# Two moved calls in the attention loop: the first turn of cached keys, and the scores of the samples

## The chip, the cores and the metric

The kernel runs on one core of a Trainium2 chip. The core has five engines with an instruction queue each: TensorE (PE, matrix products; its weight loads are shown apart as PEld), VectorE (DVE), ScalarE (ACT), GpSimd (POOL) and SyncE (SP, which here issues nearly all transfers). They run side by side and wait for each other through semaphores. The metric is the device time of one execution in microseconds (us), the median of several.

## The reference, cut to what matters

Two layers of a hybrid decoder run for 256 prompt tokens and for 32 sample tokens (8 sequences of 4). Each layer mixes tokens in three ways, of which dilated attention is one, and projects all three back. What the changed lines compute:

```python
for g in range(ATT_N_GROUPS):                      # three groups, dilations 1, 4, 16
    qg = rms_norm(att[:, :, g, 0], q_norm[g])
    kg = rms_norm(att[:, :, g, 1], k_norm[g])
    vg = att[:, :, g, 2]
    if kv_bufs is None:                            # prompt
        o, lse = dilated_attention_prompt(qg, kg, vg, ATT_DILATIONS[g])
    else:                                          # samples: keys and values from a cache
        o, lse = dilated_attention_sample(qg, kg, vg, kv_bufs[g], ATT_DILATIONS[g])
    outs.append(o)
    lses.append(lse)
wts = jax.nn.softmax(jnp.stack(lses), axis=0)
y_att = jnp.sum(wts[..., None] * jnp.stack(outs), axis=0)
...
mixed = (gates[:, :, 0] * (y_hg @ w_out_hg)
         + gates[:, :, 1] * (y_ssm @ w_out_ssm)
         + gates[:, :, 2] * (y_att @ w_out_att))
```

A query sees 129 keys per group at the distances 0, dil, ..., 128 dil. A feed-forward stage follows, dense in layer 0 and with 8 experts in layer 1.

## The kernel before

Every engine's instructions are written out in order by hand; nothing reorders them later. Where two engines share a buffer, the later one waits for a semaphore. All products land in eight PSUM banks (2 KB per partition each). A table (`job(key, b)`) gives each result its bank; `open_bank(key)` makes PE wait until the previous content of that bank has been read out ("drained"), `close_bank` tells the readers that it is filled.

The changed loop stands in `mixer` on PE and runs once in each of the two layers. It makes four passes, n = 0, 2, 4, 6. A pass handles two heads of a block of 128 prompt queries (n and n + 1) and the cached keys of two sample sequences (n and n + 1):

- `scores(L, n, k)`: six products for two heads against the prompt's key block k, one head into bank 0 and one into bank 1. Passes 0 and 4 have only block 0 (`blocks_of(n)` is 1), passes 2 and 6 have blocks 0 and 1. Both blocks use the same two banks, so block 1 waits until DVE has read block 0 out.
- `sample_keys(L, b, k)`: turns (transposes) a part of sequence b's cached keys, k = 0 to 3, into banks 5, 6, 5, 6. Part 0 is two turns, the others are four each. Part 0 waits for the transfers of that sequence's cache (semaphore k_in). DVE reads parts 0 and 1 out, ACT parts 2 and 3.
- `sample_scores(L, pair)`: the sample queries against the turned keys of the two sequences of the pass before, into banks 7 and 3, which stay open over all four passes. It waits until all eight parts of these keys have been read out.
- `turn_weights`: turns the prompt's softmax weights, in banks 2 and 0; `weigh(L, n - 2)`: multiplies the weights of the pass before with the values, into bank 4.
- `out_tile(0, m)`, `out_tile(1, m)`: a 128-wide tile of the output projection of the two other branches, eight matmul rows in the trace, mostly in bank 1, which it shares with the second head's scores. They are work that PE can do while the softmax runs.

DVE's order (`prompt_scores`, the call for even n) in a pass is: read out the scores of block 0 of both heads with scale and mask (line 2780), then those of block 1 if there is one; the row maxima (2785, 2786); the key parts 0 and 1 of sequence n out of banks 5 and 6 (2766, 2768); the two sums' reciprocals and the scaling of the weights (2791, 2792), behind ACT's exponentials; and then `gated(0, n)`, which reads the out tile from bank 1 and multiplies it with its gate (2463). For odd n it is key parts 0 and 1, and `gated`. ACT's order is: the exponentials of both heads, key parts 2 and 3 of sequence n, the turned weights, key parts 2 and 3 of sequence n + 1. A key's buffers are three sequences deep. SP loads the caches of sequences 0 to 2 ahead of the loop, and that of sequence b after part 3 of sequence b - 3 has been turned.

PE's products all go through the helper line 1036 and its full-width turns through line 1042, so the trace tells them apart by shape: scores have 64-row weights, sample scores `128*32` weights, `weigh` `128*64` weights, out tiles `128x288`. A float32 product is two matmul rows in the trace, a turn is one.

Of the kernel before, what the change touches and what calls it, by code (L numbers as in the profile page):

```python
# [93 lines left out]
def hybrid_decoder(nc, x_prompt, x_sample, state_hgrn, state_ssm, state_conv, cache_kv_w128, cache_kv_w512,  # L94
# [6 lines left out]
    with ctx:  # L101
# [252 lines left out]
        def blocks_of(n):  # L354

            return 1 + n // 2 % 2
# [155 lines left out]
        def drained(key):  # L512
            b, n = jobs[key]
            return bank_drained[b], n + 1
# [33 lines left out]
        def cache_buffer(which, b):  # L548
            return (VALUE_BUFFER if which else KEY_BUFFER)[b]

        def cache_in(L, which, b):

            order = KEY_BUFFER + VALUE_BUFFER
            n = DB * which + b
            i = order[n]
            return k_in[i], 64 * (L * order.count(i) + order[:n + 1].count(i))
# [461 lines left out]
        def _(pe):  # L1018
# [4 lines left out]
            def open_bank(key):  # L1023

                b, n = jobs[key]
                assert opened[b] == n, key
                opened[b] += 1
                if n > 0:
                    pe.wait_ge(bank_drained[b], n)
                return bank[b]  # L1030

            def close_bank(ins, key):
                ins.then_inc(bank_filled[jobs[key][0]], 1)

            def put(out, lhsT, rhs, start=True, stop=True):
                return mm(out, lhsT, rhs, start=start, stop=stop, skip_group_check=True)  # L1036

            def turn(out, in_):

                k, m = in_.shape  # L1040
                if m == P:
                    return nc.tensor.transpose(out, in_, ident[0:k, 0:k])  # L1042
                return put(out, in_, ident[0:k, 0:k])
# [13 lines left out]
            def run(products):  # L1057
                for _ in products:
                    pass
# [27 lines left out]
            def mean_over_features(L, which):  # L1087
                acc = open_bank(("norm", L, which))
                pe.wait_ge(*at_norm("x_summed", L, which))
                close_bank(put(acc[:, 0:T], ones[:, :], hT[:, 0, :]), ("norm", L, which))  # L1090
# [332 lines left out]
            def scores(L, n, k):  # L1423

                j, tb = n // 4, n // 2 % 2
                both = [open_bank(("sc", L, n + e, k)) for e in range(2)]
                for g in range(AG):
                    for e in range(2):
                        r = slice(64 * e, 64 * e + 64)
                        ins = put(both[e][:, P * g:P * g + P], att[r, 4 * g + j, P * tb:P * tb + P],  # L1430
                                  att[r, 4 * g + 2 + j, P * k:P * k + P])
                        if g == AG - 1:
                            close_bank(ins, ("sc", L, n + e, k))
# [28 lines left out]
            def sample_keys(L, b, k):  # L1462

                rows, far = kb_rows[cache_buffer(0, b)], kb_far[cache_buffer(0, b)]
                acc = open_bank(("kT", L, b, k))
                if k == 0:
                    pe.wait_ge(*cache_in(L, 0, b))
                    for p in range(2):
                        ins = turn(acc[:, P * p:P * p + P], rows[:, 0, P * p:P * p + P])
                elif k < 3:  # L1470
                    for i in range(4):
                        r, p = 2 * (k - 1) + i // 2, i % 2
                        ins = turn(acc[:, P * i:P * i + P], rows[:, 1 + r, P * p:P * p + P])
                else:
                    for i in range(4):
                        ins = turn(acc[:, P * i:P * i + P], far[:, i // 2, P * (i % 2):P * (i % 2) + P])
                close_bank(ins, ("kT", L, b, k))
# [118 lines left out]
            def mixer(L):  # L1596
                for t in range(N_PROJ):
                    run(proj_tile(L, t))
                    if t == 0:
                        pe.wait_ge(consts_ready, 2)  # L1600
                        mean_over_features(L, 0)
                    if t == 1 and L == 0:
                        skip_columns()
                    run(small_products(L, t))
                    if t == AT_DT:
                        pe.wait_ge(wdt_in, 16 * (L + 1))
                        step_widths(L)
                    if t == AT_DT + 2:
                        acc = open_bank(("dt_sum", L))
                        pe.wait_ge(*drained(("dt", L)))  # L1610
                        close_bank(put(acc[0:SH, 0:T], fourth[:, :], yall[:, 9, :]), ("dt_sum", L))
                kv_rows_of(L)
                def out_tile(br, m):

                    n = n_slab[0] + 2 * br + m // 4
                    if m % 4 == 0:
                        pe.wait_ge(slab_in[n % RING], 16 * slab_dmas[n])
                    key = ("out", L, br, m)
                    close_bank(contract(key, slab(n, 4, 4 * P), P * (m % 4), 4, yall[:, 4 * br:4 * br + 4, :]), key)

                pe.wait_ge(*at("hg_done", L))
                pe.wait_ge(*at("ssm_done", L))
                for n in range(0, 8, 2):
                    scores(L, n, 0)
                    sample_keys(L, n, 0)
                    sample_keys(L, n, 1)
                    if blocks_of(n) == 2:
                        scores(L, n, 1)
                    if n > 0:
                        sample_scores(L, n // 2 - 1)  # L1630
                        weigh(L, n - 2)
                    out_tile(0, n)
                    sample_keys(L, n, 2)
                    sample_keys(L, n, 3)

                    sample_keys(L, n + 1, 0)
                    turn_weights(L, n, 0)
                    sample_keys(L, n + 1, 1)
                    if blocks_of(n) == 2:
                        turn_weights(L, n, 1)  # L1640
                    out_tile(0, n + 1)
                    turn_weights(L, n + 1, 0)
                    sample_keys(L, n + 1, 2)
                    if n < 6:
                        out_tile(1, n // 2)
                    if blocks_of(n) == 2:
                        turn_weights(L, n + 1, 1)
                    sample_keys(L, n + 1, 3)
                weigh(L, 6)
                sample_scores(L, 3)  # L1650
                for m in (3, 4, 5):
                    out_tile(1, m)
                sample_weights(L)
                out_tile(1, 6)
                sample_new_values(L)
                for pair in range(4):
                    sample_values(L, 2 * pair)
                    sample_values(L, 2 * pair + 1)
                    if pair > 0:
                        sample_heads(L, pair - 1)  # L1660
                sample_heads(L, 3)
                out_tile(1, 7)
                pe.wait_ge(*drained(("att_o", L, 1)))
                pe.wait_ge(*drained(("oT", L)))
                if L == DEPTH - 1:
                    pe.sem_inc(loop_signals["m_slab"], 16)
                n_slab[0] += 4
                proj_slab(L, [("out", L, 2, m) for m in range(KT)], 2, yall[:, 8:10, :])
                for s in range(NS_WO):
                    w = take_slab(KT, 256)  # L1670
                    for i in range(2):
                        key = ("wo", L, 2 * s + i)
                        acc = open_bank(key)
                        for k in range(KT):
                            if s == 0 and i == 0:
                                pe.wait_ge(*at("mixed_ready", L, k + 1))
                            ins = put(acc[:, 0:T], w[:, k, P * i:P * i + P], yall[:, k, :], k == 0, k == KT - 1)
                        close_bank(ins, key)
                        if L == DEPTH - 1 and s == 0 and i == 0:
                            pe.sem_inc(loop_signals["m_slab"], 2)  # L1680
                        m = 2 * s + i
                        if L == DEPTH - 1 and m > 0:
                            router_tile(m - 1)
                    n_slab[0] += 1
                if L == DEPTH - 1:
                    router_tile(KT - 1)
# [1672 lines left out]
```

## Time and profile before

| | us |
|---|---|
| median of 3 runs | 2120.06 (2118.96 to 2120.28) |
| profiled execution | 2119.31 |
| its span, first to last instruction | 2117.4 |
| PE busy | 2080.4 (98% of the span) |
| DVE, ACT, POOL busy | 732.1, 400.6, 102.0 |
| the changed loop in layer 0 | from 373.26 to about 431.2 |
| the changed loop in layer 1 | from 1079.93 to about 1137.9 |

In the timeline, a row is a merged group: its start and length in us, engine, line, operation, output and input tile, shape and count. In brackets stands how long the engine was idle before it, and who ended the idle time. `1.00` as PEclk is TensorE's full clock of 2.4 GHz.

### The profile page before, as it was taken

The page shows a single profiled execution, that of the slowest core. Times are in us where ns is not written, and L with a number is a line of the kernel's source. Part 1 is how long each engine was busy: PE and PEld are TensorE (multiplying, and loading weights), DVE is VectorE, ACT ScalarE, POOL GpSimd, SP SyncE. Part 2 cuts the span into 40 slices and gives each one's busy share as a digit, 9 for nine tenths or more (in the row PEclk, how much of TensorE's full clock was granted, in tenths as well). Part 3 has the DMA queues.
Part 4 walks back from the last instruction along what each step waited for, and adds up shares of the span by engine and source line. Part 5 has one row for each costly group of instructions (what it writes and reads, how often), then busy time and mean ns, then how long its engine had stood idle before and what let it go on. Part 6 is the DMA issues. An engine that isn't in the chain of part 4 may idle for free.

```text
span 2117.4 us, 45520 instructions
## 1 busy us (share of the span) xinstructions
PE 2080.4 (98%) x20233; PEld 1333.8 (63%) x20233; DVE 732.1 (35%) x1435; ACT 400.6 (19%) x760; POOL 102.0 (5%) x158
## 2 busy tenths in 40 slices
PE   7999999999999999999999999999999999999998
PEld 5777777778999977777777734444343434343435
DVE  5385333545677627743254321010101010101013
ACT  3423423311220123334342120000000000000000
POOL 3000020000000000011200010000000000000001
PEclk9999999999999999999999999999999999999999
DMA  5433634785554543454467689999999999999996
GB/s 166 130 110 117 187 114 131 216 250 169 156 150 147 155 134 120 122 155 135 148 180 209 229 348 411 410 411 410 411 412 409 414 407 415 394 417 400 410 411 251
DMA packets 287523, 548.79 MB, mean 259 GB/s; under 512 B 12793, under 2 KB 217979, under 8 KB 270880
## 3 DMA queue, kind: packets, MB, share of 16 engines
q1 hardware_dynamic: 279340, 535.85, 70.0%
q10 hardware_dynamic: 6644, 5.58, 0.9%
q0 software_dynamic: 1344, 4.45, 0.6%
q8 instruction: 160, 2.62, 0.5%
q14 instruction: 35, 0.29, 0.0%
HBM read 527.15 MB, written 22.50 MB: 260 GB/s over the span
## 4 chain that ended last, share of the span: by engine, by line
PE 94%; DVE 2%; issue 1%; POOL 1%; ACT 1%; DMA 1%; POOLq 0%; DVEq 0%; ACTq 0%
PE bank L1036 92%; PE bank L1042 3%; DMA mem<-yslots,mem 1%; ACT mem L1989 1%; DVE mem L2459 0%; DVE mem L2780 0%; DVE mem L2463 0%; POOL quarterm L911 0%; DVE hflat L2492 0%; POOL mem L992 0%; DVE mem L2806 0%; POOL lmask L887 0%; POOL lmask L889 0%; DVE col L2813 0%; DVE hflat L2459 0%
## 5 line engine op out<-in xcount | busy, mean ns | idle before, releaser
L1036 PE MATMUL bank<-mem 128*32 128x256 f32 (+10 forms) x12904 | 1047.7, 390 | 14.5 <-issue 5.7
L1036 PEld LDWEIGHTS bank<-mem 128*32 128x32 f32 (+2 forms) x12904 | 636.5, 126 | 408.4 <-issue 234.7
L1036 PE MATMUL bank<-hflat,mem 128*128 128x288 f32 (+4 forms) x2784 | 629.8, 385 | 2.3 <-DVE xT L3323 1.6
L1036 PEld LDWEIGHTS bank<-hflat,mem 128*128 128x128 f32 (+2 forms) x2784 | 479.4, 188 | 125.5 <-issue 15.2
L1989 ACT ACTIVATE mem<-bank 128x288 f32<-128x288 f32 (+5 forms) x411 | 175.7, 432 | 842.4 <-PE bank L1036 780.9
L1036 PE MATMUL bank<-mem,steps 128*32 128x384 f32 (+1 forms) x3072 | 289.8, 539 | 0.0
L1036 PEld LDWEIGHTS bank<-mem,steps 128*32 128x32 f32 x3072 | 94.8, 110 | 191.7 <-issue 190.9
L2459 DVE TENSOR_TENSOR mem<-mem 128x512 f32<-128x512 f32 (+10 forms) x280 | 192.3, 713 | 28.6 <-PE bank L1036 18.5
L2463 DVE SCALAR_TENSOR_TENSOR hflat<-hflat,bank 128x512 f32<-128x512 f32 x24 | 15.1, 682 | 411.2 <-ACT hflat L1989 411.2
L1989 ACT ACTIVATE hflat<-bank 128x512 f32<-128x512 f32 (+1 forms) x40 | 19.6, 553 | 563.9 <-PE bank L1036 563.9
L1989 ACT ACTIVATE mem<-mem 128x1152 f32<-128x1152 f32 (+9 forms) x125 | 92.1, 738 | 107.0 <-DVE mem L2537 71.4
L2463 DVE SCALAR_TENSOR_TENSOR mem<-mem,bank 128x288 f32<-128x288 f32 (+1 forms) x73 | 34.1, 485 | 138.4 <-ACT mem L1989 100.1
L1042 PE MATMUL bank<-ident,mem 128*128 128x128 f32 (+3 forms) x459 | 63.8, 279 | 12.7 <-DMA mem<-in_x_sample_dram 7.1
L1042 PEld LDWEIGHTS bank<-ident,mem 128*128 128x128 f32 (+3 forms) x459 | 52.6, 143 | 26.7 <-issue 11.5
L1989 ACT ACT_TABLE_LOAD x41 | 52.6, 1283 | 17.6 <-issue 10.8
L2466 DVE SCALAR_TENSOR_TENSOR mem<-mem,bank 128x384 f32<-128x384 f32 (+2 forms) x45 | 18.4, 438 | 107.6 <-PE bank L1036 106.9
L2459 DVE TENSOR_TENSOR mem<-mem,bank 128x256 f32<-128x256 f32 (+2 forms) x92 | 37.5, 407 | 35.3 <-PE bank L1036 32.7
L992 POOL DMA_INDIRECT mem<-yslots,mem x6 | 5.9, 978 | 837.8 <-PE bank L1036 836.2
L2466 DVE SCALAR_TENSOR_TENSOR hflat<-hflat,bank 128x512 f32<-128x512 f32 x24 | 15.1, 683 | 85.5 <-PE bank L1036 85.5
L2463 DVE SCALAR_TENSOR_TENSOR mem<-mem 128x288 f32<-128x288 f32 (+3 forms) x45 | 25.5, 566 | 30.5 <-ACT mem L1989 29.1
L2616 DVE SCALAR_TENSOR_TENSOR mem<-mem,vecs 128x312 f32<-128x312 f32 x48 | 26.1, 544 | 1.7
L2554 DVE COPY_PREDICATED mem<-lmask,bank 128x512 f32<-128x512 uint32 (+1 forms) x32 | 21.6, 676 | 11.7 <-PE bank L1036 10.7
(242 smaller groups left out, 699.2 us busy)
## 6 DMA issues: line engine op xcount, KB each, us to landing
mem<-in_w_moe_up_dram SPq DMA_DIRECT2D x64, 2048.0 KB, 19.9
mem<-in_w_moe_down_dram SPq DMA_DIRECT2D x56, 2048.0 KB, 20.8
mem<-in_w_moe_up_dram SPq DMA_DIRECT2D x32, 2304.0 KB, 22.0
mem<-in_w_in_dram SPq DMA_DIRECT2D x70, 1024.0 KB, 5.2
mem<-in_w_moe_up_dram SPq DMA_DIRECT2D x16, 1536.0 KB, 20.8
mem<-in_w_ffn_up_dram SPq DMA_DIRECT2D x44, 512.0 KB, 5.2
mem<-in_cache_kv_w_dram SPq DMA_DIRECT2D x26, 512.0 KB, 5.0
mem<-in_cache_kv_w_dram SPq DMA_DIRECT2D x74, 128.0 KB, 4.8
```

What stands on the lines that cost most here:

```text
L992: return gp.indirect_dma_start(dst, None, src, bass.IndirectOffsetOnAxis(ap=slots, axis=0), bounds_check=last_row, oob_is_err=False)
L1036: return mm(out, lhsT, rhs, start=start, stop=stop, skip_group_check=True)
L1042: return nc.tensor.transpose(out, in_, ident[0:k, 0:k])
L1989: return nc.scalar.activation(out, in_, f, **kw)
L2459: return ve.tensor_tensor(out, a, b, op)
L2463: return ve.scalar_tensor_tensor(out, tanh, 1.0, b, ALU.add, ALU.mult)
L2466: return ve.scalar_tensor_tensor(out, a, 0.5, b, ALU.mult, op)
L2554: empty(ve.copy_predicated(a[0:n], mk, src), key)
L2616: ins = ve.scalar_tensor_tensor(cv[:, m, 0:CW], xpad[:, m, j:j + CW], w[j], cv[:, m, 0:CW], ALU.mult, ALU.add)
```

## The change

It changes PE's order alone, in all four passes of the loop in both layers. The first turn group of the sequence's keys (part 0) now stands ahead of the pass's first score block. The sample scores of the pass before, which stood behind the second score block, now stand ahead of it (in passes 0 and 4, which have no second block, they keep their place). No product, transfer, wait condition or bank is added or taken away; the other engines' order stays.

```diff
                 for n in range(0, 8, 2):
+                    sample_keys(L, n, 0)
                     scores(L, n, 0)
-                    sample_keys(L, n, 0)
                     sample_keys(L, n, 1)
+                    if n > 0:
+                        sample_scores(L, n // 2 - 1)
                     if blocks_of(n) == 2:
                         scores(L, n, 1)
                     if n > 0:
-                        sample_scores(L, n // 2 - 1)
                         weigh(L, n - 2)
                     out_tile(0, n)
```

In these lists a row is one kind of product with its count; six rows of `128x128` from `mem` are a score block, `ident` marks a turn.

PE at the start of pass 0, with the semaphores that each row waits for:

```order
 L1036 MATMUL bank<-ident,mem 32x128 [waits bank_drained3]
 L1036 MATMUL bank<-ident,mem 32x128 x3
-L1036 MATMUL bank<-mem 128x128 [waits bank_drained0,bank_drained1,ssm_done,hg_done]
+L1042 MATMUL bank<-ident,mem 128x128 [waits bank_drained5,k_in0,ssm_done,hg_done]
+L1042 MATMUL bank<-ident,mem 128x128
+L1036 MATMUL bank<-mem 128x128 [waits bank_drained1,bank_drained0]
 L1036 MATMUL bank<-mem 128x128 x5
-L1042 MATMUL bank<-ident,mem 128x128 [waits k_in0,bank_drained5]
-L1042 MATMUL bank<-ident,mem 128x128
 L1042 MATMUL bank<-ident,mem 128x128 [waits bank_drained6]
 L1042 MATMUL bank<-ident,mem 128x128 x3
```

The two turns of part 0, with their wait for the cache (k_in0), moved from behind the score block to ahead of it.

PE in pass 2, where there are two score blocks (pass 6 reads alike); `32x512`, `32x256` and `32x128` are the sample scores, `64x128` is `weigh`, `128x288` the out tile:

```order
-L1036 MATMUL bank<-mem 128x128 x6
-L1042 MATMUL bank<-ident,hflat 128x128 x6
-L1036 MATMUL bank<-mem 128x128 x6
+L1042 MATMUL bank<-ident,hflat 128x128 x2
+L1036 MATMUL bank<-mem 128x128 x6
+L1042 MATMUL bank<-ident,hflat 128x128 x4
 L1036 MATMUL bank<-mem 32x512 x4
 L1036 MATMUL bank<-mem 32x256 x4
 L1036 MATMUL bank<-mem 32x128 x4
+L1036 MATMUL bank<-mem 128x128 x6
 L1036 MATMUL bank<-mem 64x128 x6
 L1036 MATMUL bank<-mem 128x288 x4
```

Two turns moved ahead of the first score block, and the second score block moved behind the twelve sample score products, so that only `weigh` stands between it and the out tile.

PE in pass 4, which has one score block:

```order
 L1042 MATMUL bank<-ident,mem 128x128 x7
 L1036 MATMUL bank<-mem 128x288 x4
-L1042 MATMUL bank<-ident,mem 128x128 x7
-L1036 MATMUL bank<-mem 128x128 x6
-L1042 MATMUL bank<-ident,mem 128x128 x6
+L1042 MATMUL bank<-ident,mem 128x128 x9
+L1036 MATMUL bank<-mem 128x128 x6
+L1042 MATMUL bank<-ident,mem 128x128 x4
 L1036 MATMUL bank<-mem 32x512 x4
 L1036 MATMUL bank<-mem 32x256 x4
```

Here only the two turns moved, to the end of the turns of the pass before.

## Rows read from the trace of the kernel before

**Rows 1.** Page, part 1: busy time of the engines.

```profile
PE 2080.4 (98%) x20233; PEld 1333.8 (63%) x20233; DVE 732.1 (35%) x1435; ACT 400.6 (19%) x760; POOL 102.0 (5%) x158
```

**Rows 2.** Windows: stretch, PE, PEld, DVE, ACT, POOL busy, PEclk, DMA, GB/s.

```profile
373.20:431.20 58.00, 54.47 (x430) 41.45 (x428) 33.33 (x71) 22.23 (x45) 2.38 (x3) 1.00 0.68 200
1079.80:1137.80 58.00, 54.47 (x430) 41.44 (x428) 33.34 (x71) 22.24 (x45) 2.38 (x3) 1.00 0.70 200
1232.70:1239.50 6.80, 6.09 (x32) 1.52 (x36) 0.00 (x0) 3.51 (x4) 2.04 (x2) 0.50 0.45 183
```

**Rows 3.** Waits from 373 to 431: total us, times, longest.

```profile
PE bank L1036 <- DVE mem L2780: 1.7, 3, 0.6
...
PE bank L1042 <- ACT mem L1989: 1.0, 3, 0.3
...
PE bank L1036 <- DVE mem L2463: 0.5, 2, 0.3
```

**Rows 4.** Timeline, layer 0, start of pass 0: start, us, engine, what.

```profile
373.26 0.94 PE L1036 MATMUL bank<-mem 64*128 64x128 f32 x12
...
374.13 0.87 PE L1042 MATMUL bank<-ident,mem 128*128 128x128 f32 x6
...
374.34 1.15 DVE L2780 SCALAR_TENSOR_TENSOR mem<-bank,amask 128x384 f32<-128x384 f32 x2 [2.99 <-PE bank L1036]
...
375.63 2.18 PE L1036 MATMUL bank<-mem 128*128 128x288 f32 x8 [0.63 <-DVE mem L2780]
```

**Rows 5.** Timeline, layer 0, pass 2.

```profile
385.87 0.94 PE L1036 MATMUL bank<-mem 64*128 64x128 f32 x12 [0.27 <-DVE mem L2463]
...
386.87 1.15 DVE L2780 SCALAR_TENSOR_TENSOR mem<-bank,amask 128x384 f32<-128x384 f32 x2 [1.14 <-PE bank L1036]
...
388.17 5.53 PE L1036 MATMUL bank<-mem 64*128 64x128 f32 x56 [0.55 <-DVE mem L2780]
389.18 1.15 DVE L2780 SCALAR_TENSOR_TENSOR mem<-bank,amask 128x384 f32<-128x384 f32 x2 [1.16 <-PE bank L1036]
...
391.48 1.75 PEld L1036 LDWEIGHTS bank<-mem 128*128 128x128 f32 x8 [0.17 <-issue]
...
392.71 0.42 DVE L2766 COPY mem<-bank 128x256 f32<-128x256 f32 x1
...
393.17 0.69 DVE L2768 COPY mem<-bank 128x512 f32<-128x512 f32 x1
...
393.53 1.04 PE L1042 MATMUL bank<-ident,hflat 128*128 128x128 f32 x8
...
394.23 1.23 ACT L1989 ACTIVATE mem<-bank 128x512 f32<-128x512 f32 x2 [0.43 <-PE bank L1042]
...
394.88 1.62 PE L1042 MATMUL bank<-ident,mem 128*128 128x128 f32 x12 [0.31 <-ACT mem L1989]
...
395.60 0.45 DVE L2463 SCALAR_TENSOR_TENSOR mem<-mem,bank 128x288 f32<-128x288 f32 x1
...
396.33 2.11 PE L1036 MATMUL bank<-mem 128*128 128x288 f32 x8
```

**Rows 6.** Timeline, layer 0, start of pass 4, and a run of 14 turns.

```profile
402.23 0.94 PE L1036 MATMUL bank<-mem 64*128 64x128 f32 x12 [0.20 <-ACT mem L1989]
...
403.10 0.87 PE L1042 MATMUL bank<-ident,mem 128*128 128x128 f32 x6
...
403.90 0.16 PEld L1036 LDWEIGHTS bank<-mem 128*32 128x32 f32 x8 [0.17 <-issue]
...
405.54 1.29 PEld L1036 LDWEIGHTS bank<-mem 128*64 128x64 f32 x24 [0.20 <-issue]
...
429.60 1.69 PE L1042 MATMUL bank<-ident,mem 128*128 128x128 f32 x14
```

**Rows 7.** Timeline of SP; then, of the transfers issued 367.35 to 368.0, time to landing.

```profile
366.74 1.27 SPq L721 DMA_DIRECT2D mem<-in_cache_kv_w_dram  x2
```
```profile
mem<-in_cache_kv_w_dram SPq DMA_DIRECT2D x2, 128.0 KB, 4.4
```

## The prediction

> **What bounds the kernel now.** I read the busy times first: PE is busy for 98% of the span and the others are far below [rows 1], so a change in PE's order is worth what it does to PE's idle time and no more. Next come the windows of the two loops: each is 58.0 us long, PE is busy for 54.47 us in both, the clock is at its full level, and the two layers agree to 0.01 us [rows 2]. So I work out layer 0 and take it twice. The 3.5 us that are left in a loop are partly named by the waits [rows 3]: 1.7 us for DVE's reading of scores (line 2780), 1.0 us for ACT's copies of keys, 0.5 us for DVE's gating (line 2463). Passes 0, 2 and 6 each hold one of the first kind, and the question is which of these waits the new order really removes, and which it makes. The timeline answers that, if one follows DVE as well as PE: DVE is idle for long before it gets scores, and then runs back to back.
>
> **Durations I need.** A score block takes 373.26 to 374.13, 0.87 us [rows 4]. Six turns between two other shapes take 403.10 to 403.90, 0.80 us, and one turn more or less is (1.69 - 1.04) / 6 = 0.11 us [rows 5, 6]; so four turns there take 0.58 and two 0.36. Sample scores take 403.90 to 405.54, 1.64 us [rows 6]. Pass 2 ran second score block, sample scores and `weigh` from 388.17 to 391.48, 3.31 us [rows 5], so `weigh` is 3.31 - 0.87 - 1.64 = 0.80. From the start of a score block to DVE's start on it: 389.18 - 388.17 = 1.01 us. From the end of DVE's reading (390.33, 388.02 or 375.49) to PE's start: 375.63 - 375.49 = 0.14 us [rows 4, 5].
>
> **Pass 0: a loss of 0.36 us.** The two turns now stand ahead of the scores, where PE had no idle time before 373.26 [rows 4]. The scores start 0.36 us later, DVE's 1.15 us of reading too, and the out tile, which shares bank 1 and waited for exactly that (0.63 us idle), starts at 375.99 instead of 375.63. The turns behind the scores are fewer, but that only makes the idle time longer. Bounds: 0.22 if the extra change of shape costs nothing, 0.36 as in the row; I take the row. By the Trainium skill (TensorEngine Tiling (Array Packing), Key Properties) changing the tiling mode, not just the tile, drains TensorE. The trace agrees that changes of shape cost something: 0.80 us for six turns with a change on either side, against 0.65 at 0.11 each [rows 6]. With that rule pass 0 costs 0.36 and the sum is as below; if a change were free, pass 0 would cost 0.22 and the two layers 0.3 us less.
>
> **Pass 4: a gain of 0.22 us.** The scores wait until 402.23 for ACT (0.20 us idle [rows 6]). The two turns take 0.22 us of PE and fall into this gap; the scores start when they did, and everything behind them starts 2 x 0.11 = 0.22 us earlier. DVE's part is done long before PE asks for it, since this pass has one block only. Bounds 0.1 (if the turns push the scores out by part of it) and 0.22.
>
> **Passes 2 and 6: the two obvious waits go, and come back larger.** Before: the first scores start at 385.87 after 0.27 us idle for bank 1, the second block at 388.17 after 0.55 us [rows 5]. After, step by step:
> - The two turns fill the 0.27 us gap; the first scores start at 385.87 as before, since DVE sets that.
> - Four turns follow at 386.74, sample scores at 387.32, the second block at 388.96. DVE has finished block 0 at 388.02, so nobody waits. That is the gain. But the second block starts 388.96 - 388.17 = 0.79 us **later** than before.
> - `weigh` starts at 389.83 and ends at 390.63. The out tile needs bank 1, that is the second head's block 1. DVE starts on it at 389.97 and is done at 391.12; the out tile starts at 391.26 instead of 391.48. Of the 0.85 us that PE had won, 0.63 is a new wait here, in place of the sample scores that used to cover it.
> - From here DVE's whole chain is 0.79 us late: maxima, exponentials on ACT beside it, copies of key parts 0 and 1. It was hardly early before: part 1 was read out at 393.17 + 0.69 = 393.86, and PE wanted bank 6 for part 3 at 393.53 + 4 x 0.11 = 393.97. Now part 0 is out at 393.13 + 0.79 = 393.92, while PE is there at 391.26 + 2.05 = 393.31: 0.65 us of waiting. Part 3's bank is free at 394.65, another 0.25 us.
> - ACT copies part 2 out 0.70 us after its turns start, takes 0.6, and PE's next turns start at about 395.3 instead of 394.88. The scaled weights and then `gated` come from DVE, 0.79 us late: line 2463 ends at 396.05 + 0.79 = 396.84, so the next out tile, which needs bank 1, starts at 396.98 instead of 396.33. That is the latest of the conditions: a loss of 0.65 us.
> - The rest of the pass is paced by PE, so the loss stays. The first scores of the next pass follow PE's own out tile through DVE or ACT, so no slack takes it up.
>
> Bounds: if DVE's lateness went through whole, 0.8; if only ACT's chain counted, 0.42. I take 0.65 for pass 2 and, as its rows have the same distances, for pass 6.
>
> **The sum.** Per layer 0.36 + 0.65 - 0.22 + 0.65 = 1.44 us, for two layers 2.9 us, which I round to 3.0 because each late wait also starts a new row of turns (six turns are recorded at 0.87 us [rows 4], eight at 1.04 [rows 5], and 1.04 - 2 x 0.11 = 0.82, so a first turn costs 0.05 more). The profiled execution took 2119.31 us (2117.4 of span and 1.9 around it) and lies 0.75 us under the median; against it the sum gives 2122.3, against the median 2123.1. Past the loop, both layers go on with PE as the bound, so the shift arrives at the end undiminished. SP's loads are chained to PE's turns and shift with them.
>
> **Rivals.**
> - *The waits simply vanish.* If DVE's chain had slack of 0.8 us, the out tile's 0.22 us a pass and the pass 4 gain would stand, and PE would keep nearly 0.85 us in passes 2 and 6: 0.36 - 0.85 - 0.22 - 0.85 = -1.56 us a layer, 2117.0. For it: the named waits of lines 2780 and 2463 do end. Against it: the slack is 0.1 us, by the rows above. It decides at the bank 5 and 6 turns behind the first out tile. Chance 0.07.
> - *Half and half:* DVE's lateness is partly taken up (the second block starts earlier than I have it, as the four turns or the sample scores overlap with their neighbours). The second block then decides, at 388.6 rather than 388.96; passes 2 and 6 lose 0.2 each, and the time is 2120.6 to 2121. Chance 0.12.
> - *Slower, by more than can be overlooked:* DVE's chain is the true bound of passes 2 and 6 from the second block to the end of the pass, so all of the 0.8 us goes through, and each of four new waits a pass (out tile, part 2, part 3, next part 0) restarts PE 0.1 us late. Then a pass loses 1.0 us, a layer 0.36 - 0.15 + 2.0 = 2.2, and the time is 2124.5. It decides when the out tile at 396.33 starts over 0.85 us late. For it: DVE runs without a pause from 389.18 to 396.05. Against it: the second half of the pass has PE work that waits for nobody. Chance 0.13.
> - *The cache comes too late:* the first turn of pass 0 now runs 0.87 us earlier and waits for all transfers of sequence 0. The last two are issued from 366.74 to 368.01 and take 4.4 us [rows 7], so they land near 372.4; the turns are due at 373.26. There are 0.9 us to spare; late by as much again, it would cost 1 us, 2124. Chance 0.02.
> - *The clock falls.* The loop would hold idle pieces of 0.65 us. Today it holds pieces of 0.63 and 0.55 us [rows 4, 5] at the full clock of 2.4 GHz, and the trace has a stretch of 6.8 us at 1.2 GHz, behind layer 1's mixing [rows 2]. Such a stretch over this loop would add up to half its length, 3.4 us: 2126.5. Against it: the pieces hardly grow. Chance 0.02.
>
> **How the numbers follow.** My own case (2121.9 to 2124.0 with the error of a 3-run median) has 0.64. A measurement of this kernel can tell about 0.2%, 4.2 us, from no change, that is, under 2115.8 or over 2124.3. My case, the half case and the vanishing waits at 2117.0 are all inside. Over it lie most of the slower rival, the clock and the edge of my case: 0.17. Faster by over 0.2% would need the vanishing waits and more: 0.02. The range of 8 in 10 runs from 2120.2, which takes in the half case, to 2124.9 in the slower one.
>
> **What would show it.** In the trace after: (1) no PE idle before the second block in passes 2 and 6, and DVE's second pair of line 2780 about 0.8 us later after the first pair (3.1 us instead of 2.31); (2) a new wait of about 0.6 us on line 2780 before the out tile of passes 2 and 6; (3) waits of turns on lines 2766 and 2768; (4) pass 0's wait on line 2780 grows from 0.63 to about 1.0 us, pass 4's 0.20 us is gone; (5) pass 2 begins 0.36 us later than now against the start of the loop, pass 4 about 1.0, the end about 1.4. PE's waits for line 2780 falling with no others growing would prove me wrong, and so would a loop of under 58 us.

## The result, and the profile after

| | us |
|---|---|
| before, median of 22 runs | 2119.79 (2118.09 to 2123.96) |
| after, median of 22 runs | 2123.82 (2120.42 to 2126.82) |
| ratio after to before | 1.0016 (95% interval 1.0009 to 1.0023) |
| loop in layer 0, before and after | 57.96 and 59.55 |
| loop in layer 1, before and after | 57.95 and 59.54 |

The change makes the kernel slower by about 3.4 us, 0.16%, by the ratio (its interval is 1.9 to 4.9 us); the two medians differ by 4.0 us. I measure a loop from PE's first row after the last value turn to the first row of the last `weigh`: before 373.26 to 431.22, after 373.25 to 432.80 in layer 0, and 1082.27 to 1141.81 in layer 1 of after. The two loops together are 3.2 us longer, which lies within that interval.

PE's timeline of after, layer 0, passes 0 to 4, with DVE's and PE's weight load rows where they matter. The weight load row of 389.34 is the second score block and `weigh`, 12 products or 24 rows. Line numbers above 1625 are shifted by one, so 2781, 2767, 2769, 2464 and 1990 are the 2780, 2766, 2768, 2463 and 1989 of before:

```profile
373.25 0.44 PE L1042 MATMUL bank<-ident,mem 128*128 128x128 f32 x2
...
373.62 0.94 PE L1036 MATMUL bank<-mem 64*128 64x128 f32 x12
...
375.99 2.18 PE L1036 MATMUL bank<-mem 128*128 128x288 f32 x8 [0.84 <-DVE mem L2781]
...
386.24 0.94 PE L1036 MATMUL bank<-mem 64*128 64x128 f32 x12
...
387.24 1.15 DVE L2781 SCALAR_TENSOR_TENSOR mem<-bank,amask 128x384 f32<-128x384 f32 x2 [1.14 <-PE bank L1036]
387.70 0.16 PEld L1036 LDWEIGHTS bank<-mem 128*32 128x32 f32 x8 [0.17 <-issue]
...
389.34 1.50 PEld L1036 LDWEIGHTS bank<-mem 64*128 64x128 f32 x24 [0.20 <-issue]
390.38 1.15 DVE L2781 SCALAR_TENSOR_TENSOR mem<-bank,amask 128x384 f32<-128x384 f32 x2 [1.99 <-PE bank L1036]
...
391.59 2.21 PE L1036 MATMUL bank<-mem 128*128 128x288 f32 x8 [0.50 <-DVE mem L2781]
...
394.40 1.38 PE L1042 MATMUL bank<-ident,hflat 128*128 128x128 f32 x8 [0.60 <-DVE mem L2767]
...
395.12 0.42 PEld L1042 LDWEIGHTS bank<-ident,hflat 128*128 128x128 f32 x4 [0.30 <-DVE mem L2769]
...
395.80 1.71 PE L1042 MATMUL bank<-ident,mem 128*128 128x128 f32 x12
...
396.81 0.46 DVE L2464 SCALAR_TENSOR_TENSOR mem<-mem,bank 128x288 f32<-128x288 f32 x1
...
397.35 2.18 PE L1036 MATMUL bank<-mem 128*128 128x288 f32 x8
...
399.37 0.93 PE L1042 MATMUL bank<-ident,mem 128*128 128x128 f32 x7
...
403.32 0.94 PE L1036 MATMUL bank<-mem 64*128 64x128 f32 x12
...
407.88 1.75 PEld L1036 LDWEIGHTS bank<-mem 128*128 128x128 f32 x8 [0.17 <-issue]
...
432.80 9.48 PE L1036 MATMUL bank<-mem 128*64 128x128 f32 x96
```

Read it against [rows 4 to 6]. In pass 0 the turns lead, and the scores and the out tile start 0.36 us later (373.62 for 373.26, 375.99 for 375.63). In pass 2 nothing is idle before the first block (386.24) nor before the second (389.34, against 388.17 with 0.55 us idle). But DVE now sits idle for 1.99 us instead of 1.16 before it gets the second block, at 390.38 instead of 389.18, and PE waits for DVE at the out tile (0.50 us) and at the turns behind it (0.60 us). Both waits are new.

The waits of the loop, where before had 1.7, 1.0 and 0.5 us [rows 3]:

```profile
PE bank L1036 <- DVE mem L2781: 1.8, 3, 0.8
...
PE bank L1042 <- DVE mem L2767: 1.2, 2, 0.6
...
PE bank L1042 <- ACT mem L1990: 0.3, 1, 0.3
```

The sum for line 2780 has hardly moved, although it was to be relieved: the waits only stand at other places now (0.84, 0.50 and 0.50 us for 0.63, 0.55 and 0.55). The key turns wait for DVE (1.2 us) where they waited for ACT, and the 0.5 us for line 2463 is gone from the list. Together these waits are 3.3 us, against 3.2 before, though the loop is 1.6 us longer: the waits by name hardly show the loss. The loop's windows, before and then after, columns as in [rows 2]:

```profile
373.26:431.22 57.96, 54.43 (x429) 41.45 (x428) 33.33 (x71) 22.20 (x45) 2.38 (x3) 1.00 0.68 200
```
```profile
373.25:432.80 59.55, 55.76 (x429) 41.22 (x428) 33.36 (x71) 22.18 (x45) 2.39 (x3) 1.00 0.67 194
```

PE's busy column grows by 1.33 us for the same products, its idle time only from 3.53 to 3.79 us. The profile books a wait in the middle of a merged row, or one shorter than the modelled end of the row before, as busy: the eight turns of 394.40 take 1.38 us, where they took 1.04, because the last four wait for DVE's line 2769 (395.12). So the starts of the rows are what to compare.

### The profile page after: what moved, and what is told of

Same layout as the page of the kernel before. It is cut to its first block, busy times and chain, and to the rows that moved or that the text cites. A ratio compares the mean times of both kernels' runs of the same rounds, so it can differ in the third digit from the quotient of the medians.

```text
span 2123.1 us, 45520 instructions
## 1 busy us (share of the span) xinstructions
PE 2086.2 (98%) x20233; PEld 1337.3 (63%) x20233; DVE 732.2 (34%) x1435; ACT 400.2 (19%) x760; POOL 101.8 (5%) x158
## 4 chain that ended last, share of the span: by engine, by line
PE 94%; DVE 3%; issue 1%; POOL 1%; DMA 1%; ACT 0%; POOLq 0%; DVEq 0%; ACTq 0%
PE bank L1036 91%; PE bank L1042 3%; DMA mem<-yslots,mem 1%; DVE mem L2460 0%; ACT mem L1990 0%; DVE col L2786 0%; DVE mem L2781 0%; POOL quarterm L911 0%; DVE hflat L2493 0%; POOL mem L992 0%; DVE mem L2807 0%; DVE mem L2464 0%; DVE mem L2769 0%; POOL lmask L887 0%; POOL lmask L889 0%
```

## The experiments

My theory: in passes 2 and 6 DVE's chain behind the second score block is nearly critical, so any delay of that block's start comes back. Rivals: the turns themselves, or changes of shape on PE, cost the time; or the waits are taken up later. Loops repeat to 0.02 us from layer to layer and from run to run, so their length in the trace decides finer than the time of a run. Each edit shifts the line numbers a little, so go by the operation: SCALAR_TENSOR_TENSOR with `amask` is DVE's reading of scores, COPY its reading of keys, TENSOR_REDUCE a maximum, ACTIVATE is ACT's.

**The first half of the change.**

```diff
-                    scores(L, n, 0)
                     sample_keys(L, n, 0)
+                    scores(L, n, 0)
```

> Only the first half of the change: part 0 of the keys ahead of the first score block; the sample scores stay behind the second block. The measure is the length of the loop in the trace, from PE's first row after the last value turn to the first row of the last weigh: 57.96 us before, 59.55 us after the whole change, in either layer. Theory (DVE's chain behind the second score block sets passes 2 and 6): pass 0 loses 0.36 us, pass 4 wins 0.22, passes 2 and 6 stay, since their second block still starts when DVE has read the first; the loop is 58.10 us and the time 0.3 us above before. Rival (the moved turns themselves do the harm, by more changes of shape on PE): the loop is over 59 us.

The loop is 430.84 - 372.73 = 58.11 us; the time is 0.9998 of before (0.9988 to 1.0009). PE's waits and ends:

```profile
372.73 0.44 PE L1042 MATMUL bank<-ident,mem 128*128 128x128 f32 x2
...
388.00 5.53 PE L1036 MATMUL bank<-mem 64*128 64x128 f32 x56 [0.77 <-DVE mem L2780]
...
430.84 3.35 PE L1036 MATMUL bank<-mem 128*64 128x128 f32 x57
```

The 0.27 us before pass 2's first block are filled, but the wait before its second block grows from 0.55 to 0.77 us: work moved into the first gap is missing in the second, as DVE ends both. The moved turns do little harm (0.15 us a loop, pass 0's loss less pass 4's gain); they are not the cause.

**The second half of the change.**

```diff
+                    if n > 0:
+                        sample_scores(L, n // 2 - 1)
                     if blocks_of(n) == 2:
                         scores(L, n, 1)
                     if n > 0:
-                        sample_scores(L, n // 2 - 1)
                         weigh(L, n - 2)
```

> Only the second half of the change: the sample scores between the two score blocks, part 0 of the keys where it was. Theory: the second block starts at 386.74 + 0.80 + 1.64 = 389.18 instead of 388.17, 1.01 us late, and DVE's whole chain with it; the out tile that before started at 396.33 starts 0.87 to 0.94 us late in passes 2 and 6, passes 0 and 4 stay; the loop is 59.7 to 59.8 us, longer than with the whole change, and the time 3.5 to 3.8 us above before. Rival (the two halves just add up): 59.55 - 0.14 = 59.41 us. Rival (the sample scores fill PE's idle time): under 57.4 us.

The loop is 432.69 - 372.87 = 59.82 us, longer than with the whole change, and the time 1.0013 of before (1.0004 to 1.0023). DVE has the second block at 389.84, 3.36 us after the first (386.48), where before it was 2.31 and in the whole change 3.14:

```profile
386.48 1.15 DVE L2781 SCALAR_TENSOR_TENSOR mem<-bank,amask 128x384 f32<-128x384 f32 x2 [1.14 <-PE bank L1036]
...
389.84 1.15 DVE L2781 SCALAR_TENSOR_TENSOR mem<-bank,amask 128x384 f32<-128x384 f32 x2 [2.21 <-PE bank L1036]
...
396.80 2.18 PE L1036 MATMUL bank<-mem 128*128 128x288 f32 x8
```

The halves do not add up; if they did, this loop would be 59.41 us, the whole change's less what the first half adds. The first half shortens by 0.22 us a pass what stands ahead of the second block, and so softens the harm of the second.

**Only DVE late, PE's order as before.**

```diff
+                if w == 2:
+                    step(ve.tensor_reduce(col[:, 0:1], rows[0], AX.X, ALU.max))
                 for e in range(2):
                     c = 4 * e
                     step(ve.tensor_reduce(col[:, c:c + 1], rows[e], AX.X, ALU.max))
```

> PE's order is that of before. DVE takes the row maximum of the first head twice in passes 2 and 6, which puts about 0.97 us (the row of 768 elements took 0.95 us) behind the second block and ahead of everything that follows. Theory: a late DVE chain alone costs what the change costs: each of passes 2 and 6 gets longer by 0.97 less the 0.14 us of slack, about 0.85 us, the loop is 59.6 to 59.8 us, the time 3.4 us above before. Rival (PE's order or its changes of shape cost the time and DVE has room): the loop stays within 0.3 us of 57.96.

The loop is 59.67 us. PE's turns wait for DVE as they do in the whole change, with the order of PE untouched:

```profile
389.83 0.95 DVE L2784 TENSOR_REDUCE col<-mem 128x1 f32<-128x768 f32 x1
390.81 0.95 DVE L2787 TENSOR_REDUCE col<-mem 128x1 f32<-128x768 f32 x1
...
393.64 1.38 PE L1042 MATMUL bank<-ident,hflat 128*128 128x128 f32 x8 [0.48 <-DVE mem L2766]
```

So 0.98 us of DVE's time in each of two passes costs 1.71 us of PE's in a loop: the chain has 0.1 us of slack. The time, though, was 1.0004 of before (0.9995 to 1.0014), and the 1.0016 that the loops would give lies outside that interval. The same kernel once more:

> The kernel with the row maximum taken twice, once more and with more rounds. Its loops were 59.67 and 59.68 us, 3.4 us more than before for both, but its time was only 1.0004 of before (0.9995 to 1.0014), where 3.4 us would be 1.0016. Theory (the loop's length reaches the end of the program, and the first comparison was low by the chance of the places outside it): loops 59.67 us again, ratio 1.0010 to 1.0022. Rival (something behind the loops takes the loss up when DVE alone is late): ratio under 1.0008 again.

The loop was 432.81 - 373.12 = 59.69 us again, the time 1.0007 (0.9997 to 1.0016). The estimate is on the rival's side, and the interval holds 1.0016 only at its edge. In the loop the theory stands; that the whole of the loss reaches the end of this program is not shown by its time. The last experiment below says where the rest may be.

**The whole change, and DVE reads the keys earlier.**

```diff
                 for k in range(w):
+                    if k == 1:
+                        turned_keys(L, n)
                     for e in range(2):
                         key = ("sc", L, n + e, k)
...
-                turned_keys(L, n)
+                if w == 1:
+                    turned_keys(L, n)
```

> The whole change, and DVE reads key parts 0 and 1 out between the two score blocks in passes 2 and 6 (1.11 us of reading in a stretch where it sits idle for 1.99 us), no longer behind the maxima. Theory: the turns' waits on lines 2767 and 2769 go, the weights are scaled 1.1 us earlier, and what remains is ACT, whose exponentials are still 0.8 us late and which copies part 2 only behind them: passes 2 and 6 lose 0.40 instead of 0.66 us each, the loop is 58.9 us, about 0.65 us shorter than with the change alone. Rival (DVE's chain is all there is): passes 2 and 6 lose nothing, the loop is 58.0 to 58.1 us. Rival (the new wait for bank 1 at the out tile sets the pass): 59.5 us, nothing won.

The loop is 432.00 - 373.02 = 58.98 us, the time 0.9999 of before (0.9990 to 1.0009); the loops alone would give 1.0010, just outside it. Pass 2:

```profile
388.18 0.42 DVE L2767 COPY mem<-bank 128x256 f32<-128x256 f32 x1
388.64 0.69 DVE L2769 COPY mem<-bank 128x512 f32<-128x512 f32 x1
...
394.80 1.23 ACT L1990 ACTIVATE mem<-bank 128x512 f32<-128x512 f32 x2
...
395.45 1.61 PE L1042 MATMUL bank<-ident,mem 128*128 128x128 f32 x12 [1.02 <-ACT mem L1990]
```

The copies fit into DVE's idle time, the turns' wait on DVE is gone, and ACT is next: it copies part 2 only at 394.80, behind its late exponentials, and PE waits 1.02 us for it. Of 1.59 us a loop, 0.57 came back. Of the other 1.02 us, 0.15 is the moved turns' (passes 0 and 4, as in the first experiment), and 0.87 is left in passes 2 and 6, where ACT is late, since the exponentials hang on the maxima and these on the second block.

**The other work between the two blocks.** Here `weigh`, half as long, takes the place of the sample scores, and pass 0 keeps its order.

```diff
+                    if n > 0:
+                        sample_keys(L, n, 0)
                     scores(L, n, 0)
-                    sample_keys(L, n, 0)
+                    if n == 0:
+                        sample_keys(L, n, 0)
                     sample_keys(L, n, 1)
+                    if n > 0:
+                        weigh(L, n - 2)
                     if blocks_of(n) == 2:
                         scores(L, n, 1)
                     if n > 0:
                         sample_scores(L, n // 2 - 1)
-                        weigh(L, n - 2)
```

> Order of before but for two things: weigh (0.80 us), not the sample scores (1.64 us), stands between the two score blocks, and part 0 of the keys stands ahead of the first block in passes 2, 4 and 6 but not in pass 0. Theory: four turns and weigh end at 386.74 + 0.58 + 0.80 = 388.12, just when the banks of the first block are free (388.02 + 0.14), so the second block and DVE's chain start when they did; the out tile starts 0.8 us earlier, but the turns behind it then wait for DVE, and the next out tile wins only the slack of 0.14 us. The loop is 57.96 - 2 x 0.14 - 0.22 = 57.5 us, the time 1 us under before. Rival (PE's idle time is won whole when it is filled): 57.96 - 2 x 0.8 - 0.22 = 56.1 us, 3.7 us under before.

The loop is 430.39 - 372.90 = 57.49 us, the time 0.9989 of before (0.9979 to 0.9999). DVE's two reads are 388.82 - 386.51 = 2.31 us apart, as before, so nothing is late:

```profile
386.51 1.15 DVE L2784 SCALAR_TENSOR_TENSOR mem<-bank,amask 128x384 f32<-128x384 f32 x2 [1.14 <-PE bank L1036]
...
388.82 1.15 DVE L2784 SCALAR_TENSOR_TENSOR mem<-bank,amask 128x384 f32<-128x384 f32 x2 [1.16 <-PE bank L1036]
...
392.83 1.38 PE L1042 MATMUL bank<-ident,hflat 128*128 128x128 f32 x8 [0.30 <-DVE mem L2770]
```

**The same, with DVE's earlier reading.** The diff is the one of the fourth experiment on top of the fifth.

> As e5, and DVE reads key parts 0 and 1 out between the two score blocks of passes 2 and 6, where it sits idle for 1.16 us and the reading takes 1.11. Theory: the turns no longer wait for DVE, ACT's exponentials (done at 393.80) and its copy of part 2 are next: PE's turns start at 394.49 instead of 394.88, the next out tile 0.36 us earlier. The loop is 57.96 - 2 x 0.36 - 0.22 = 57.0 us, the time 1.9 us under before. Rival: the reading pushes DVE's second block, the loop is as in e5 or longer.

The loop is 430.38 - 373.32 = 57.06 us, the time 0.9987 of before (0.9978 to 0.9996). ACT is what PE waits for:

```profile
394.61 1.62 PE L1042 MATMUL bank<-ident,mem 128*128 128x128 f32 x12 [0.78 <-ACT mem L1993]
```

This is the best version that I have: 0.9 us less in each loop than before, and a time below that of before. The two loops account for 1.8 of the 2.8 us that the ratio gives (in the fifth experiment for 0.9 of 2.3); the rest is not shown to come from the change.

**Only DVE's earlier reading, PE's order as before.**

> PE's order is that of before; only DVE's changes: key parts 0 and 1 are read out between the two score blocks of passes 2 and 6. Theory: DVE's chain gets 1.1 us of slack behind the second block, but in before nothing of PE waits for it there, ACT's copy of part 2 sets the turns (0.31 us wait), so the loop stays at 57.96 us within 0.1. Rival (DVE's chain is what bounds passes 2 and 6 of before already): the loop gets shorter by up to 2 us.

The loop stayed at 57.96 us, the time at 0.9996 (0.9987 to 1.0006). DVE's slack alone is worth nothing, because in before PE's turns wait for ACT's copy, and that is not earlier:

```profile
393.95 1.23 ACT L1989 ACTIVATE mem<-bank 128x512 f32<-128x512 f32 x2 [0.37 <-PE bank L1042]
394.60 1.61 PE L1042 MATMUL bank<-ident,mem 128*128 128x128 f32 x12 [0.31 <-ACT mem L1989]
```

**Both kernels again, for what lies outside the loops.** The profile of after has a span of 2123.1 us, 5.7 us over that of before, where the loops explain 3.2.

> The kernel of before, unchanged, for one more profile. The loops' lengths repeat to 0.05 us between layers and kernels so far, but other places do not: the profile of the changed kernel has a stretch of 6.8 us at 1.2 GHz in layer 1's output projection (from 1170.1) that the profile of before lacks, worth about 2.9 us, which is the greater part of what its span is longer beyond the two loops. Theory (that stretch is a matter of the single execution): some of these four profiles have it, of either kernel, and the loop is 57.96 us. Rival (the changed order causes it): both profiles of before lack it and both of the changed kernel have it.

> The changed kernel, unchanged, for one more profile. Theory: its loop is 59.55 us again, and the stretch at 1.2 GHz in layer 1's output projection comes or not as it does for the kernel of before. Rival: it is there again.

> The kernel of before once more. Theory: loop 57.96 us, the stretch at 1.2 GHz by chance. Rival: no such stretch.

> The changed kernel once more. Theory: loop 59.55 us, the stretch at 1.2 GHz by chance. Rival: the stretch is there.

The loops were 57.96 to 57.97 us for before and 59.53 to 59.54 us for after. The windows from 1163 to 1175, layer 1's output projection, columns as in [rows 2]; in order the first repeat of before, the first and the second of after, and the doubled maximum's second run:

```profile
1163.00:1175.00 12.00, 11.07 (x74) 8.67 (x67) 7.27 (x19) 0.00 (x0) 0.80 (x1) 1.00 0.52 166
```
```profile
1163.00:1175.00 12.00, 10.30 (x85) 7.51 (x86) 3.37 (x9) 0.00 (x0) 0.80 (x1) 0.77 0.48 143
```
```profile
1163.00:1175.00 12.00, 10.31 (x87) 7.59 (x87) 3.82 (x11) 0.00 (x0) 0.80 (x1) 0.86 0.50 150
```
```profile
1163.00:1175.00 12.00, 10.80 (x97) 8.51 (x98) 5.87 (x15) 0.00 (x0) 0.79 (x1) 1.00 0.59 177
```

The third figure from the end is the granted clock. It is below 1 in all three profiles of after and at 1.00 in all three of before, which is the rival's picture and not my theory's. Over all profiles: with a changed order on PE, seven of eight have a piece at 1.2 GHz there (after three times, and the first, second, fifth and sixth experiment; the fourth has none); with PE's order of before, none of six (before three times, the doubled maximum twice, DVE's earlier reading). The doubled maximum shifts this stage by as much as the change does and has no such piece. What the piece costs can be read from its stage: from the first row of layer 1's last `weigh` to the first row behind the output projection, before takes 45.5 to 46.4 us and after 47.7 to 49.0. Behind that stage it turns round: to the end of the program before takes 933.2 to 936.6 us and after 932.6 to 933.0, as two of the three profiles of before have another piece at 1.2 GHz, from about 1219, which those of after lack. Over the whole trace such pieces add up to 13.7, 17.1 and 20.5 us in before and to 13.7, 13.6 and 10.2 us in after, so the changed kernel is not at the lower clock for longer.

Outside the loops, that is with both loops taken off the span, before has 2001.5 to 2003.9 us, after 2002.5 to 2004.1, and all kernels 2000.9 to 2005.3. What this piece has to do with an order 30 us earlier I cannot say; it stays open, and so does whether anything outside the loops adds to the measured difference, for which its interval leaves room up to 1.7 us. The doubled maximum lies at the low end there (2000.9 and 2001.2), which may be where its missing time is.

## Why the prediction was right, point by point

- **The bound.** Following DVE as well as PE, from start to start of the rows, was the right method: a count of the named waits would have promised 0.8 us a pass. That a change is worth what it does to PE's idle time "and no more" does not hold for the idle time that the profile gives, which grew by 0.26 us in a loop that grew by 1.59.
- **Pass 0**, 0.36 us lost: measured 375.99 - 375.63 = 0.36.
- **Passes 2 and 6**, 0.65 us each: 397.35 - 396.33, less the 0.36 us inherited, is 0.66, and pass 6 lost 0.65 (429.19 for 427.66, with 0.88 inherited). The steps too: the second block 1.17 us after before's with 0.36 of it inherited, that is 0.81 (0.79 foreseen); the out tile at 391.59, foreseen at 391.26 + 0.36 = 391.62; the turns at 394.40, foreseen at 393.92 + 0.36 = 394.28; the gating's end at 397.27, foreseen at 396.84 + 0.36 = 397.20. The one step that the sum left out: the out tile that starts right behind DVE's read-out takes 2.02 us to the next turns (397.35 to 399.37), where it had followed PE's own turns and taken 1.94 (396.33 to 398.27 before), another 0.07 us in pass 2 and 0.05 in pass 6. Why it takes longer is not shown. I had rounded 2.9 up to 3.0 for restarted rows of turns, not for this; the loops show 3.2. The rows of before, for this and for pass 4:

```profile
398.27 0.93 PE L1042 MATMUL bank<-ident,mem 128*128 128x128 f32 x7
...
407.00 1.75 PEld L1036 LDWEIGHTS bank<-mem 128*128 128x128 f32 x8 [0.17 <-issue]
```

- **Pass 4**, 0.22 us won: the out tile's weight load is at 407.88, 4.56 us behind the first scores (403.32), where it was 4.77 us (407.00 and 402.23): 0.21.
- **The sum**, 3.0 us, was 3.2 in the loops and 3.4 (1.9 to 4.9) in the time. The loops bear it out; the time is too coarse for that. That the forecast 2123.1 and the median 2123.82 are so close is in part luck: the forecast stood on a median of 2120.06 where that of 22 runs is 2119.79, and what lies outside the loops differs by 2.4 us between profiles of one and the same kernel (before).
- **The way to the end.** Between the loops the shift passes whole: from loop to loop it is 648.7 to 649.7 us in before and 648.7 to 649.5 in after. Behind the second loop the pieces at the lower clock hide whether it arrives undiminished.
- **The rivals.** The vanishing waits and the half case fell by the loop of 59.55 us. The slower rival has the right mechanism and too high a price (1.0 us a pass for 0.7); PE's free work at the end of a pass did not take up any of the loss, and did not add to it either but for those 0.07 us. The caches were not late: the turn of 373.25 started without a wait. A piece at the lower clock was to be in the loop; none was there, but there was one later on.
- **What would show it:** all five signs came. (1) 3.14 us between DVE's reads. (2) The new wait at the out tile, 0.50 us by the profile's figure, about 0.6 foreseen. (3) Turns waiting on 2767 and 2769. (4) No idle time before pass 4's scores, and a longer wait in pass 0, but of 0.84 us and not of about 1.0: I had added the whole 0.36 us to 0.63, though the moved turns put off not only DVE's reading but also the end of the turns ahead of the wait, by 0.15 us (375.15 for 375.00), so that 0.21 was due. (5) Pass 2 begins 0.38 us later against the start of the loop, pass 4 1.10 and the end 1.59, for 0.36, 1.0 and 1.4.

## What to carry to other kernels

To fill a gap in which an engine waits for a partner, take work that is just as long as the gap; here 0.80 us of `weigh` in the gap of 0.77 us that the first experiment left made nobody late and won 0.1 us in passes 2 and 6 each (0.3 with DVE's copies moved into DVE's own gap), and 1.64 us of sample scores lost 0.66. What follows the gap feeds the partner's next stretch, so read from the partner's timeline how much later it may start: its slack, not the idle time of the filled engine, is the budget. And ask what the moved work used to cover where it stood, here the wait for the bank that the second block and the out tile share. Last, compare the starts of rows and not the idle sums: of PE's loss of 1.59 us a loop, 1.33 stood in its busy column.

## What the runs showed of the hardware that I had not expected

In layer 1's output projection TensorE's clock was at 1.2 GHz for 3.4 to 10.2 us in seven profiles, while PE was busy most of the time: from 1168.50 to 1175.50 in the profile of after, with a mean granted clock of 0.61, PE has 6.29 us of 7.00 in its busy column.

```profile
1168.50:1175.50 7.00, 6.29 (x20) 4.28 (x20) 2.07 (x8) 0.00 (x0) 0.79 (x1) 0.61 0.27 71
```

Ahead of it PE had gone through the sample values with short waits (0.49 and 0.22 us in the timeline of after). They do not tell the two cases apart: the first repeat of before has 0.52 and 0.22 us at the same rows, and its clock stayed at 2.4 GHz. The eight rows of an out tile that begin just ahead of it take 3.28 us, where the same row took 2.19 us in the profile of before. After, then the first repeat of before:

```profile
1165.64 1.30 PE L1036 MATMUL bank<-mem 128*32 128x64 f32 x40 [0.49 <-issue]
...
1168.15 1.06 PE L1036 MATMUL bank<-tmask,mem 128*128 128x8 f32 x8 [0.22 <-DVE mem L2460]
1169.06 3.28 PE L1036 MATMUL bank<-mem 128*128 128x288 f32 x8
```
```profile
1162.43 1.30 PE L1036 MATMUL bank<-mem 128*32 128x64 f32 x40 [0.52 <-issue]
...
1164.94 1.06 PE L1036 MATMUL bank<-tmask,mem 128*128 128x8 f32 x8 [0.22 <-DVE mem L2459]
```

Also, from the end of DVE's read-out to PE's start it was 0.14 us in pass 0 (375.85 and 375.99) but 0.06 us in pass 2 (391.53 and 391.59), where I had taken 0.14 for all; behind a plain copy it was 0.06 (394.34 and 394.40).
